# Another order for the steps of the grid layer: gate rows in steps 1 and 2, gate projections done by step 9, two row tiles turned in step 12

## The reference, cut to what matters

```python
# even_layer: 256 rows of x (hl) and 256 rows of context (hc), 1024 wide
q, k, v, u, vv, gate = jnp.split(hl @ w_in, EVEN_SPLITS, axis=-1)     # the same for hc
a  = windowed_sink_gqa(rope(q), rope(k), v, kc, vc, sink)             # 8 heads of 64
b  = chunk_gmlp(gelu(u), gelu(vv), ln_g, ln_b, w_s, b_s)              # gelu(u) * (w_s @ layer_norm(gelu(vv)) + b_s)
y  = (jnp.concatenate([a, b], axis=-1) * jax.nn.silu(gate)) @ w_out
# second_block
shift, scale, gate = jnp.split(cond @ w_ada[layer] + b_ada[layer], 3, axis=-1)
x  = x + gate * y                                                     # a row vector per layer and condition
```

## Time and profile before

| | us |
|---|---|
| median of 3 runs (1145.53 to 1147.34) | 1146.91 |
| the profiled execution | 1148.03 |
| its span | 1146.2 |
| PE busy in it | 1093.0 |
| even layer's attention, first gate projection to last output projection (in the trace) | 770.4 to 948.3 |

### The profile page before, as it was taken

One profiled execution on the slowest core, in us unless ns is written; L12 is line 12 of the kernel. 1 busy time (PEld: TensorE's weight loads), 2 busy tenths in 40 slices (PEclk: granted clock), 3 DMA queues, 4 the chain that ended last, 5 costly groups with the idle time before them and its releaser, 6 DMA issues.

```text
span 1146.2 us, 12963 instructions
## 1 busy us (share of the span) xinstructions
PE 1093.0 (95%) x5022; PEld 724.0 (63%) x5022; DVE 538.8 (47%) x1107; ACT 427.1 (37%) x878; POOL 96.0 (8%) x115
## 2 busy tenths in 40 slices
PE   4999999999999999999999999999898999999997
PEld 2787775644446877755544467777576787346773
DVE  2439766552425397742143244235634554236643
ACT  2436545320024365463300153353635423325431
POOL 3004110000000041100000000400000001230000
PEclk9999999999999999999999999999899999999999
DMA  9653333567314533333565342530551016242000
GB/s 384 246 210 151 147 148 114 205 268 293 148 58 178 214 151 147 147 147 147 225 238 213 130 187 82 189 116 1 221 195 49 1 37 232 80 153 86 2 1 37
DMA packets 13740, 171.25 MB, mean 149 GB/s; under 512 B 1504, under 2 KB 1760, under 8 KB 3056
## 3 DMA queue, kind: packets, MB, share of 16 engines
q1 hardware_dynamic: 12944, 167.77, 38.4%
q10 hardware_dynamic: 736, 2.65, 0.6%
HBM read 169.37 MB, written 1.05 MB: 149 GB/s over the span
## 4 chain that ended last, share of the span: by engine, by line
PE 83%; DVE 6%; ACT 6%; DMA 3%; issue 1%; ACTq 0%; DVEq 0%
PE bank L723 18%; PE bank L745 11%; PE bank L1061 8%; PE bank L1019 7%; PE bank L1067 7%; PE bank L1108 6%; PE bank L715 5%; PE bank L1285 2%; PE bank L1301 2%; PE bank L823 2%; DVE wlo L2060 2%; PE bank L678 2%; PE bank L686 2%; DMA ring<-in_weights 1%; DMA X<-in_x 1%; PE bank L1142 1%
## 5 line engine op out<-in xcount | busy, mean ns | idle before, releaser
L723 PE MATMUL bank<-ring,hT 128*128 128x512 f32 (+1 forms) x576 | 243.5, 578 | 1.1 <-ACT retqkv L1341 0.6
L723 PEld LDWEIGHTS bank<-ring,hT 128*128 128x128 f32 x576 | 107.3, 190 | 120.1 <-issue 114.0
L2060 DVE TENSOR_TENSOR wlo<-ring,whi 128x512 fp32r<-128x512 f32 x120 | 89.0, 767 | 40.5 <-ACT whi L1417 40.4
L745 PE MATMUL bank<-whi,xhi 128*128 128x512 f32 (+1 forms) x256 | 99.2, 387 | 6.6 <-DVE wlo L2060 4.7
L1417 ACT ACTIVATE whi<-ring 128x512 fp32r<-128x512 f32 x120 | 72.6, 630 | 64.3 <-PE bank L745 64.0
L745 PE MATMUL bank<-whi,xlo 128*128 128x512 f32 (+1 forms) x256 | 96.5, 377 | 0.0
L745 PE MATMUL bank<-wlo,xhi 128*128 128x512 f32 (+1 forms) x256 | 96.4, 376 | 0.0
L1067 PE MATMUL bank<-ring,hT 128*128 128x512 f32 (+2 forms) x288 | 85.8, 457 | 3.2 <-ACT hT L1384 2.3
L1067 PEld LDWEIGHTS bank<-ring,hT 128*128 128x128 f32 x288 | 50.9, 190 | 35.8 <-issue 29.7
L745 PEld LDWEIGHTS bank<-whi,xhi 128*128 128x128 f32 x256 | 48.1, 188 | 21.4 <-issue 7.7
L1341 ACT ACTIVATE G<-bank 128x512 f32<-128x512 f32 x24 | 14.3, 596 | 119.7 <-PE bank L723 119.7
(11 more groups left out here) (403 smaller groups left out, 1774.1 us busy)
## 6 DMA issues: line engine op xcount, KB each, us to landing
ring<-in_weights SPq DMA_DIRECT2D x73, 2048.0 KB, 8.4
ring<-in_weights SPq DMA_DIRECT2D x5, 1024.0 KB, 5.1
ring<-in_weights SPq DMA_DIRECT2D x2, 1360.0 KB, 7.9
ring<-in_weights SPq DMA_DIRECT2D x1, 1536.0 KB, 9.8
kk<-in_k SPq DMA_DIRECT2D x1, 1120.0 KB, 8.1
X<-in_x ACTq DMA_DIRECT2D x1, 1024.0 KB, 16.2
kc<-in_k ACTq DMA_DIRECT2D x1, 1024.0 KB, 11.7
X<-in_context SPq DMA_DIRECT2D x1, 1024.0 KB, 10.6
```

Source lines behind the costliest of these rows:

```text
L723: mm = pe.matmul(ps[:, 0:width], hT[:, k, t * P:(t + 1) * P], ring[:, slot, k * stride + w0:k * stride + w0 + width], start=(k == 0), stop ...
L745: mm = pe.matmul(o[:, 0:width], a, b[:, q % BUFFERS, at], start=(k == 0 and m == 0), stop=(k == KD - 1 and m == 2))
L2060: dve.tensor_tensor(wlo1[:, q % BUFFERS, :], piece1(q)[2], whi1[:, q % BUFFERS, :], ALU.subtract).then_inc(event("lo1_ready"), 1)
```

## The change

It moves work between steps and leaves the set of PE products as it is.

- **Loads.** adag4 and adag5 (the chunks of the gate vector) are loaded where ada0 and ada1 were, within the split projections ahead of the attention. ada0 to ada3 follow later. ada0 now waits for the fourth gate projection (step 3) and no longer for the spatial product; e_o0 comes ahead of ada2 and e_o1; ada3 goes to the slot of e_g1.
- **Gate rows.** DVE builds both diagonals ahead of the layer norm, in rows of `eg` that are still unused; PE does `gate_rows` in steps 1 and 2 (before: 12 and 13).
- **First gate projection.** PE's wait for ACT's copies of the turned queries and keys comes after the first gate projection, not ahead of it.
- **Gates.** The second half of the gate is projected in steps 6 to 9 (before: 7, 8, 10, 11), its Silu is in step 10 (before: 12) and that of the first half in step 6 (before: 5). ACT's four high pieces of e_g1 are all in step 3, DVE's rests in step 4; those of e_o0 in steps 10 and 11.
- **Spatial product** in step 5 (before: 4). The sums are in steps 6, 7, 9, 13.
- **Mixing.** DVE gates row tile 1 and mixes tiles 0 and 1 in step 11, and PE turns them in step 12, into banks 4, 5, 0, 1, freed by DVE's `mixed_low`. Tiles 2 and 3 are turned between the first output projections.

```diff
-CHE = [("e_kv", KD * 256, 0), ("e_q", KD * 512, 1), ("e_u", KD * 512, 2), ("ada0", KD * 512, 0), ("e_vv", KD * 512, 1),
-       ("e_g0", KD * 512, 0), ("ada1", KD * 512, 2), ("e_ws", KD * P, 2), ("e_g1", KD * 512, 1), ("ada2", KD * 512, 2),
-       ("adag4", KD * 512, 0), ("ada3", KD * 512, 2), ("adag5", KD * 512, 0), ("e_o1", KD * 512, 2), ("e_o0", KD * 512, 0)]
+CHE = [("e_kv", KD * 256, 0), ("e_q", KD * 512, 1), ("e_u", KD * 512, 2), ("adag4", KD * 512, 0), ("e_vv", KD * 512, 1),
+       ("e_g0", KD * 512, 0), ("adag5", KD * 512, 2), ("e_ws", KD * P, 2), ("e_g1", KD * 512, 1), ("ada0", KD * 512, 0),
+       ("ada1", KD * 512, 2), ("e_o0", KD * 512, 0), ("ada2", KD * 512, 2), ("e_o1", KD * 512, 2), ("ada3", KD * 512, 1)]
...
-E_GATES = {0: 0, 1: 1, 2: 2, 3: 3, 7: 4, 8: 5, 10: 6, 11: 7}
-E_EARLY = {6: "ada0", 10: "ada1"}
-E_SUMS = {6: "ada2", 7: "adag4", 8: "ada3", 9: "adag5"}
-E_ADA = {7: "ada2", 8: "adag4", 9: "ada3", 10: "adag5"}
+E_GATES = {0: 0, 1: 1, 2: 2, 3: 3, 6: 4, 7: 5, 8: 6, 9: 7}
+E_EARLY = {6: "adag4", 10: "adag5"}
+E_SUMS = {6: "ada0", 7: "ada1", 9: "ada2", 13: "ada3"}
+E_ADA = {7: "ada0", 8: "ada1", 10: "ada2", 14: "ada3"}
...
-E_ROWS_AT = {12: 0, 13: 1}
+E_ROWS_AT = {1: 0, 2: 1}
+E_SPATIAL, E_TURNED = 5, 12
...
-        DG2 = evv[:, 2:4, :].rearrange("p t (k c) -> p (t k) c", k=KD // 2)
+        DG2 = [eg[:, 2 + v, :].rearrange("p (k c) -> p k c", k=KD) for v in range(2)]
...
@@ PE: the copies of eqT and ekT are waited for in step 0, behind the gate projection
-            for j in range(2):
-                emptied(pe, u, f"ekT{j}")
-            for j in range(4):
-                emptied(pe, u, f"eqT{j}")
+                if g == 0:
+                    for j in range(2):
+                        emptied(pe, u, f"ekT{j}")
+                    for j in range(4):
+                        emptied(pe, u, f"eqT{j}")
+                if g == E_TURNED:
+                    turn_mixed(0)
+                    turn_mixed(1)
@@ ACT
-                if g in (5, 12):
-                    n = g // 7
+                if g in (6, 10):
+                    n = g // 10
-                for j, n in {4: ((1, 0), (1, 1)), 5: ((1, 2), (1, 3)), 11: ((2, 0), (2, 1)), 12: ((2, 2), (2, 3))}.get(g, ()):
+                for j, n in {3: ((1, 0), (1, 1), (1, 2), (1, 3)), 10: ((2, 0), (2, 1)), 11: ((2, 2), (2, 3))}.get(g, ()):
                     wide_high(j, n)
@@ DVE
+            for v in range(2):
+                diagonal(DG2[v], v)
...
+                if g == 11:
+                    e_gated(1)
...
+                    e_mixed(0)
+                    e_mixed(1)
+                    wide_low(2, 0)
+                    wide_low(2, 1)
+                if g == E_TURNED:
+                    wide_low(2, 2)
+                    wide_low(2, 3)
+                    mixed_low(0)
+                    mixed_low(1)
+                    e_mixed(2)
+                    e_mixed(3)
```

More of the change, by code:

```diff
@@ L246, in units_of_layer_e @@
                     u.append((f"eo{t}", 2 + t % 2))
-        if g == 4:
+        if g == E_SPATIAL:
             u += [(f"gs{j}", proj()) for j in range(4)]
[L249 to L254, removed]
+        if g == E_TURNED:
+            u += [(f"eyT{t}{h}", (4, 5, 0, 1)[2 * t + h]) for t in range(2) for h in range(2)]
+    u += [(f"eyT{t}{h}", (4, 5, 0, 1)[2 * t + h - 4]) for t in range(2, NT) for h in range(2)]
+    u += [(f"eout{t}0", (6, 7, 2, 3)[t]) for t in range(NT)]
+    u += [(f"eout{t}1", (4, 5, 0, 1)[t]) for t in range(NT)]
     return u
@@ L522, in e_rows @@
         def e_rows(name):
-            return eg[:, int(name[-1]), 0:512] if name in E_EARLY.values() else msum2[E_ROWS.index(name) % 2]
+            return eg[:, int(name[-1]) - 4, 0:512] if name in E_EARLY.values() else msum2[E_ROWS.index(name) % 2]
         def e_which(name):
@@ L1165, in e_logits_pair, with turn_mixed @@
                             done(u, f"el{i}", mm)
+            def turn_mixed(t):
+                pe.wait_ge(event("em_ready"), t + 1)
+                pe.wait_ge(event("eb_ready"), t + 1)
+                for h in range(2):
+                    ps = begin(u, f"eyT{t}{h}")
+                    done(u, f"eyT{t}{h}", turn_blocks(ps, [eg[:, t, (4 * h + i) * P:(4 * h + i + 1) * P] for i in range(4)]))
             for g in range(E_STEPS):
@@ L1614, in wide_high, with mixed_high @@
                 act.activation(whole, w, ACT.Copy).then_inc(event("wide_high"), 1)
+            def mixed_high(t):
+                for h in range(2):
+                    ps = filled(act, u, f"eyT{t}{h}")
+                    act.activation(xhi[:, 4 * h:4 * h + 4, t * P:(t + 1) * P], ps[:, :].rearrange("p (k c) -> p k c", k=4),
+                                   ACT.Copy).then_inc(event("yhi_ready"), 1)
             def e_sums_out(name):
@@ L1633, in _ @@
                 split_high(q)
-            ada_out(u, "ada0", e_rows("ada0"))
+            ada_out(u, "adag4", e_rows("adag4"))
             for q in range(8, 10):
@@ L1641, in _ @@
                 split_high(q)
-            ada_out(u, "ada1", e_rows("ada1"))
+            ada_out(u, "adag5", e_rows("adag5"))
             for i in range(2, 4):
@@ L1692, in _ @@
                         copy_out(u, f"gb{v}{h}", gbr[:, v, h * 512:(h + 1) * 512])
+                if g == E_TURNED:
+                    mixed_high(0)
+                    mixed_high(1)
                 for t in range(NT):
[L1694 removed]
+                    if g == E_LAST[t] // 2 + (t < NT - 1):
                         act.wait_ge(event("e_arg"), t + 1)
                         act.activation(es2[:, t, :], es2[:, t, :], ACT.Exp).then_inc(event("e_es"), 1)
[L1697 to L1706 removed]
+            mixed_high(2)
+            mixed_high(3)
+            for i in range(4):
+                wide_high(3, i)
             X_O = [1, 2, 3, 4]
@@ L2381, in _ @@
                 if q == 9:
-                    mod_out(u, "ada0", 0, e_which("ada0"), (1, 2))
+                    mod_out(u, "adag4", 4, e_which("adag4"), (1, 2))
                 if q >= 10:
@@ L2424, in e_gated, with mixed_low @@
                 dve.wait_ge(event("em_ready"), t + 1)
+            def mixed_low(t):
+                for h in range(2):
+                    dve.wait_ge(event("yhi_ready"), 2 * t + h + 1)
+                    ps = filled(dve, u, f"eyT{t}{h}")
+                    c = slice(t * P, (t + 1) * P)
+                    dve.tensor_tensor(xlo[:, 4 * h:4 * h + 4, c], ps[:, :].rearrange("p (k c) -> p k c", k=4),
+                                      xhi[:, 4 * h:4 * h + 4, c], ALU.subtract).then_inc(free(u, f"eyT{t}{h}"), 1)
             def e_mixed(t):
@@ L2472, in _ @@
                         ins.then_inc(free(u, f"gs{j}"), 1)
-                for j, n in {5: ((1, 0), (1, 1)), 6: ((1, 2), (1, 3)), 12: ((2, 0), (2, 1))}.get(g, ()):
-                    wide_low(j, n)
-                if g in (8, 11):
-                    e_gated((g - 8) // 3)
-                if g == 13:
+                if g == 4:
+                    for n in range(4):
+                        wide_low(1, n)
+                if g == 8:
+                    e_gated(0)
+                if g == 11:
+                    e_gated(1)
                     for j in range(4):
```

67 lines of the change are left out of this document (18 added, 49 removed).

## The result

The changed kernel takes 1158.95 us in the median of 4 runs (1157.71 to 1164.11), the kernel before, over all 4 of its runs up to then, 1146.22 (1144.78 to 1147.34). The ratio is 1.0122, interval 1.01 to 1.0143: slower by 1.2%. The forecast was 1164 us, range 1151 to 1171.

A forecast was written before the change was run, and what follows sets the result against it. PE bounds the kernel, busy 1093 of 1146.2 us. New waits 22.8, plus clock 13.8, less 0.6 and 18.75 gone, make +17.25 us: forecast 1164 us, own range 1156 to 1171, 8-in-10 range 1151 to 1171.

The forecast's parts named there:

- The 18.75 us: Even layer: 12.2 us of four old PE waits plus 6.55 us of slow-clock work behind three, all predicted to go.
- A1: Step 1, second gate row: PE waits 3.0 us for a bank ACT copies only after step 0's exponentials.
- A3: Step 3: projection waits 4.65 us for a gate row's bank, copied by ACT behind the exponentials of step 2.
- A2: Step 2: projection waits 4.65 us for bank0, whose gate row ACT copies behind both exponentials of step 1.
- A4: Step 5: wait of 2.95 us behind ACT's four high pieces, the spatial product no longer standing in between.
- A5: Step 11, last logits: wait of 2.65 us, ACT having Silu and table loads ahead of step 10's copies and exponentials.
- the rival of the dearer table switch: Table switches cost more, A5 at twice its size with its clock: 1167 us; chance 0.03.
- A6: Step 13: sums of ada3 wait 4.9 us for bank0, full until DVE's third mixed_low.
- The clock: Slow-clock work behind each of the six new waits, 13.8 us in sum, bounds 0 to 17.7.
- six dips: Sign: granted clock shows six dips between 784 and 915 us, where the kernel before had three.
- priced by the nearest row: Slow work priced from old waits: 2.9 us for A2, A3, A6; 1.8 for A1, 1.7 for A4, 1.6 for A5.
- The rival of the other side: Gate rows don't stall: A1 to A3 and their clock go, 1144 us, 0.25% faster; chance 0.05.

The follow-up runs named there:

- e9_rows0_spatial4: Changed kernel with both gate rows in step 0, ACT's copies of them ahead of the exponentials, and the spatial product back in step 4: 1136.56 us, ratio 0.9918.
- e8_best: e9_rows0_spatial4 with second-half Silu behind the last exponentials, mixed rows turned a step later, ada3's sums a step earlier, DVE's e_o0 rests split in pairs: 1130.46 us.
- b1_eq_wait: Kernel before, with only PE's wait for the turned queries and keys moved behind the first gate projection: 1145.9 us, ratio 0.9994.
- e1_gbr_first: Changed kernel with ACT copying the gate rows right behind the gate projection's copy, ahead of the exponentials, in steps 1 and 2: 1151.58 us, ratio 1.0038.
- e3_spatial4: Changed kernel with the spatial product back in step 4 instead of step 5: 1154.14 us, ratio 1.007.
- e5_silu_late: Changed kernel with the Silu of the gate's second half behind the exponentials of step 10, not ahead of them: 1160.28 us, ratio 1.012.
- e10_busy11: e9_rows0_spatial4 with 11 small unread matmuls of ones on PE ahead of the logits of step 11: 1138.81 us, ratio 0.9936.
- e4_dve_order: Changed kernel with DVE's four rests of e_o0 behind the rests of the two turned tiles in step 12, not ahead: 1158.88 us, ratio 1.0104.
- e7_rows0: Changed kernel with both gate rows in step 0 and ACT's copies of them ahead of the exponentials: 1144.04 us, ratio 0.9976.

## Why the prediction was right, point by point

**Work, and what is gone.** Right. PE's work is the same, all four old waits went, and no load came in their place in the kernel after. The 18.75 us hold to within 1 us in the accounts of e9_rows0_spatial4 and e8_best. One part of them had a condition that I had not named: the 2.5 us at the turned queries go only if PE has work until DVE is through with the layer norm. In b1_eq_wait 1.9 of them came back.

**A1 to A3** (3.0, 4.65, 4.65): 3.22, 4.53, 4.54. The mechanism was the one named, as e1_gbr_first shows for A2 and A3. A1 was not changed by itself; that PE waited there for ACT's copy of `eg` is read from its releaser. Both sides of that race came 1 us later than worked out, as the whole attention did. A3's chain, logits to projection, is 5.67 us (803.32 to 808.99) for 5.7. A2's is 6.57, since the logits ahead of it stood in A1's slow stretch (2.04 us for 1.13), and the wait stayed the same because PE's side grew with it.

**A4 and A5** (2.95, 2.65): 2.62 and 2.62. A4 by the four pieces that the spatial product had covered (e3_spatial4), A5 by the Silu with its two tables (e5_silu_late moves it away, and A5 falls to 0.2). ACT in steps 3 and 10 of the kernel after:

```profile
822.95 3.88 ACT L1616 ACTIVATE wide<-ring 128x1024 fp32r<-128x1024 f32 x4
...
884.21 1.28 ACT L1676 ACT_TABLE_LOAD   x1
885.50 1.91 ACT L1676 ACTIVATE eg<-eg 128x2048 f32<-128x2048 f32 x1
887.32 1.07 ACT L1343 ACTIVATE hT<-bank 128x512 f32<-128x512 f32 x2
888.40 1.28 ACT L1691 ACT_TABLE_LOAD   x1
```

A switch costs its 1.28 us and 0.01 behind it (884.21 + 1.28, then 885.50), so the rival of the dearer table switch falls. By the rule of the Trainium skill (page "ScalarE: Activation LUTs", section "What ACT_TABLE_LOAD costs") A5 would have been 5.4 us; the trace doesn't agree, with 2.62.

**A6** (4.9, less 0.6 for the clock): 2.18. Here the step on DVE's chain was right and that on PE's side was mis-sized. From the logits of step 11 to the sums of ada3 it is 12.85 us (891.77 to 904.62), for 12.55. PE's side was 10.7 us for 7.65: the slow stretch behind A5, which cost 3.3 us, lies wholly within it. I had priced that stretch at 1.6 us, like the shortest of rows 4, and let only 0.6 of it count here. In e10_busy11, without that stretch, the wait is 5.05 us, close to the 4.9 of the undisturbed race.

**The clock** (13.8): 10.2. That waits of this size are followed by slow work was right five times in six. The sign I had named, six dips, came out as four, since A1 and A2 share one: when A2 begins the clock is already down, so of the two waits of 4.5 us only A3 shows a dip of its own. By size they were 1.0, 1.8, 2.5, 1.7, 3.3 and nothing, for 1.8, 2.9, 2.9, 1.7, 1.6 and 2.9. The mis-sized step is "priced by the nearest row": ordering the stretches by the length of the wait ahead of them. The 2.62 us of A4 had 4.0 us of slow stretch behind them in after and 12.6 in e1_gbr_first, the 2.62 us of A5 6.6 and 12.4.

**The range** of the forecast's own case, 1156 to 1171, has a slip at its lower end: with the waits 0.5 us shorter each and 1.2 us of clock for each the same sum gives 1154.6. The measured time lies within it either way.

**The sum** thus came out 5.5 us below the forecast of +17.25 in the span: clock -3.6, A6 -2.1, the other waits -0.4, and +1.2 from ahead of the attention; 0.6 is left over, the same 0.6 by which the account lies above the trace. The rival of the other side (gate rows that don't stall) needed only that ACT's copies come first; with them there and nothing else changed the time was 1151.58, since the slow stretches behind A4 and A5 grew. With both rows in step 0 it was 1144.04, at the rival's figure of 1144, but by chance, with another make-up: A6 smaller, the clock dearer.

## What to carry to other kernels

A copy that empties a PSUM bank belongs, in the queue of the engine that does it, ahead of anything that waits for a third engine: four copies of half a microsecond, put behind the exponentials, cost 9.1 us of PE's time here. When a block is moved, work out for every queue the race between the new neighbours from their common starting point, and ask of what was moved away which wait it had covered. Before working on a slow stretch or a wait, look at which chain sets the next one: time taken from in front of a wait on another engine's chain only makes this wait longer, as e4_dve_order, e5_silu_late and e10_busy11 show. And before a difference of a few microseconds between two traces is put down to an edit, see how much of it stands ahead of the edit: 3.4 of 5.0 us did in e3_spatial4.

## What the runs showed of the hardware

The length of a stretch at the lower clock isn't given by the wait ahead of it. Behind the same 2.62 us it was between 4.0 us (A4 in after) and 13.1 us (e7_rows0). Nor does every standstill have one: behind the 2.18 us of A6 in after and the 1.9 us of b1_eq_wait there is none, behind the 1.7 us of e8_best there are 3.3 us of work at 0.55. What decides whether it comes and how long it lasts, the runs leave open, and each kernel left one trace, so that its spread between executions of one kernel isn't shown. The mean granted clock of an execution doesn't stand in for it: executions of the kernel before took 1145.17 us at 0.990 and 1147.48 us at 0.993. A forecast that prices such a stretch by one row should hold both ends, here a factor of three, in its range.
